# Layer 0's gated product laid out for the out-projection by VectorE blocks and GpSimd copies, and a new order of the last eight granules

## The reference, cut to what matters

```python
def pool_layer(x, norm_g, w_in, w_pool, pool_scale, w_out):      # layer 0
    h = rms_norm(x, norm_g)
    u, z = jnp.split(h @ w_in, 2, axis=-1)                       # 2048 columns each
    y = pool_mixer(u, w_pool, pool_scale) * jax.nn.silu(z)       # windows 2, 4, 8, 16; 4 groups of 512
    return x + y @ w_out

def moba_layer(x, norm_g, w_in, q_norm, k_norm, w_out):          # layer 1
    h = rms_norm(x, norm_g)
    q, k, v, z = jnp.split(h @ w_in, 4, axis=-1)                 # 16 heads of 128 each
    q = rope(rms_norm(heads(q), q_norm))
    k = rope(rms_norm(heads(k), k_norm))
    o = causal_attention(q, k, v)                                # one block of 256 tokens
    return x + (o * jax.nn.silu(z)) @ w_out
```

## Time and profile before

| what | value |
|---|---|
| median of three executions | 426.38 us (426.24 to 426.8) |
| the profiled execution, its own time | 427.27 us |
| its span (first to last instruction) | 425.3 us |
| PE busy | 416.2 us, 98% of the span |
| DVE busy | 292.3 us, 69% |
| ACT busy | 237.0 us, 56% |
| POOL busy | 31.9 us, 8% |
| mean granted clock of TensorE | 0.992 of full |
| moved by DMA | 86.78 MB, mean 204 GB/s |

### The profile page before, as it was taken

One profiled execution on the slowest core, in us unless ns is written; L12 is line 12 of the kernel. 1 busy time (PEld: TensorE's weight loads), 2 busy tenths in 40 slices (PEclk: granted clock), 3 DMA queues, 4 the chain that ended last, 5 costly groups with the idle time before them and its releaser, 6 DMA issues.

```text
span 425.3 us, 5551 instructions
## 1 busy us (share of the span) xinstructions
PE 416.2 (98%) x2126; PEld 356.1 (84%) x2126; DVE 292.3 (69%) x373; ACT 237.0 (56%) x430; POOL 31.9 (8%) x45
## 2 busy tenths in 40 slices
PE   9999999999999999999999999999999999959997
PEld 8989898988888888888888888888888888848885
DVE  3879987779885545358934799358983699833532
ACT  5755453535454443469639785379846797443310
POOL 0175000000000000111001100011001010000000
PEclk9999999999999999999999999999999999988999
DMA  8996868453555747337694567794877927861002
GB/s 269 387 353 213 262 217 322 180 205 114 195 197 168 224 124 222 117 105 241 247 331 119 182 209 236 248 299 147 269 214 215 323 95 272 290 205 50 0 2 99
DMA packets 45945, 86.78 MB, mean 204 GB/s; under 512 B 2528, under 2 KB 8288, under 8 KB 45920
## 3 DMA queue, kind: packets, MB, share of 16 engines
q1 hardware_dynamic: 45200, 85.37, 60.4%
q10 hardware_dynamic: 720, 1.07, 0.8%
HBM read 79.61 MB, written 6.82 MB: 203 GB/s over the span
## 4 chain that ended last, share of the span: by engine, by line
PE 89%; DVE 6%; DMA 3%; SPq 0%; issue 0%; ACT 0%; DVEq 0%
PE acc L633 23%; PE acc L635 23%; PE acc L634 23%; PE acc L656 3%; PE acc L678 3%; PE acc L677 3%; PE acc L675 3%; DMA between<-uT 2%; DVE w_lo L848 2%; PE acc L697 1%; PE aux L688 1%; PE aux L772 1%; PE aux L779 1%; PE aux L771 1%; PE aux L790 1%; PE aux L791 1%
## 5 line engine op out<-in xcount | busy, mean ns | idle before, releaser
L848 DVE TENSOR_TENSOR w_lo<-raw,w_hi 128x2048 fp32r<-128x2048 f32 x65 | 147.9, 2285 | 45.2 <-ACT w_hi L384 45.2
L384 ACT ACTIVATE w_hi<-raw 128x2048 fp32r<-128x2048 f32 x64 | 122.0, 1914 | 43.9 <-PE acc L635 31.0
L633 PE MATMUL acc<-w_hi,hT_hi 128*128 128x512 f32 x320 | 126.9, 397 | 0.0
L635 PE MATMUL acc<-w_hi,hT_lo 128*128 128x512 f32 x320 | 124.8, 390 | 0.0
L634 PE MATMUL acc<-w_lo,hT_hi 128*128 128x512 f32 x320 | 124.6, 389 | 0.0
L635 PEld LDWEIGHTS acc<-w_hi,hT_lo 128*128 128x128 f32 x320 | 60.1, 188 | 12.9
L634 PEld LDWEIGHTS acc<-w_lo,hT_hi 128*128 128x128 f32 x320 | 60.2, 188 | 11.9
L633 PEld LDWEIGHTS acc<-w_hi,hT_hi 128*128 128x128 f32 x320 | 60.1, 188 | 11.7
L633 PE MATMUL acc<-w_hi,aT_hi 128*128 128x512 f32 x160 | 64.7, 404 | 4.9 <-DVE aT_lo L1067 4.9
L634 PE MATMUL acc<-w_lo,aT_hi 128*128 128x512 f32 x160 | 63.2, 395 | 0.0
L635 PE MATMUL acc<-w_hi,aT_lo 128*128 128x512 f32 x160 | 63.1, 395 | 0.0
(11 more groups left out here) (126 smaller groups left out, 452.1 us busy)
## 6 DMA issues: line engine op xcount, KB each, us to landing
raw<-in_w_in_dram SPq DMA_DIRECT2D x46, 1024.0 KB, 6.7
raw<-in_w_out_dram SPq DMA_DIRECT2D x16, 1024.0 KB, 5.3
raw<-in_w_pool_dram SPq DMA_DIRECT2D x4, 1024.0 KB, 5.4
between<-wide SPq DMA_DIRECT2D x8, 512.0 KB, 3.9
raw<-in_w_in_dram SPq DMA_DIRECT2D x8, 256.0 KB, 7.5
wide<-between SPq DMA_DIRECT2D x16, 128.0 KB, 2.8
qkT<-between SPq DMA_DIRECT2D x16, 128.0 KB, 2.9
between<-uT SPq DMA_DIRECT2D x3, 512.0 KB, 10.0
```

The lines of the kernel that those rows point to most:

```text
L384: act.activation(w_hi[:, slot, :], raw[:, slot, :], ACT.Copy).then_inc(hi_made, 1)
L633: pe.matmul(a, shi, whi, start=first and k == 0, stop=False)
L635: ins = pe.matmul(a, slo, whi, start=False, stop=last and k == GK - 1)
L848: dve.tensor_tensor(w_lo[:, slot, :], raw[:, slot, :], w_hi[:, slot, :].bitcast(F32), ALU.subtract).then_inc(w_split, 1)
```

## The change

The transposes of y0 on PE are gone. DVE turns y0 in blocks of 32x32 into `qkT[:, g % 2]`, which holds nothing else at that time, and POOL copies the sixteen 32x256 blocks of a group to their places between the partitions, into the quarter of `wide` that held the group's gate. For that the gate of group g now lies in one contiguous quarter, `quarters[:, g]`. ACT and DVE take the high and the low parts from there, in SBUF, not from PSUM. DVE's list around this is in a new order. In layer 1's out-projection the granule (1, 0) and (1, 1) stand ahead of (0, 2), and the parts of y1 of group 2 are made one round later.

```diff
-OUT1_ORDER = [(0, 0), (0, 1), (0, 2), (1, 0), (1, 1), (1, 2), (0, 3), (1, 3)]
+OUT1_ORDER = [(0, 0), (0, 1), (1, 0), (1, 1), (0, 2), (1, 2), (0, 3), (1, 3)]
...
+        def y0_blocks(g):
+            return qkT[:, g % 2].rearrange("p h s -> p (h s)")
+
+        def y0T(g):
+            return quarters[:, g].rearrange("p t n -> p (t n)").rearrange("p (h s) -> p h s", h=HPG)
...  POOL, behind the rope tables:
+            def place_blocks(dst, blocks, made):
+                for a in range(P // Q):
+                    for b in range(P // Q):
+                        to = dst[b * Q:(b + 1) * Q].rearrange("p h (t a i) -> p a t h i", t=TT, i=Q)[:, a]
+                        at = blocks[a * Q:(a + 1) * Q, b * 2 * P:(b + 1) * 2 * P].rearrange("p (t h i) -> p t h i", t=TT,
+                                                                                            h=HPG)
+                        ins = pool.tensor_scalar(to, at, 1.0, 1.0, ALU.mult, ALU.mult)
+                ins.then_inc(made, 1)
+
+            for g in range(GROUPS):
+                pool.wait_ge(y0_blocked, g + 1)
+                place_blocks(y0T(g), y0_blocks(g), y0T_made)
...  ACT:
             def y0_hi(g):
-                for b in range(2):
-                    turned_hi(aT_hi, HPG * g + 2 * b, 2 * (g % 2) + b, (y_turned, 2 * g + b + 1), y_hi, gain=2 * KD)
-
+                act.wait_ge(y0T_made, g + 1)
+                for h in range(HPG):
+                    f = HPG * g + h
+                    ins = act.activation(aT_hi[:, f, :], y0T(g)[:, h], ACT.Copy,
+                                         scale=gains[:, 2 * KD + f:2 * KD + f + 1])
+                    if h % 2:
+                        ins.then_inc(y_hi, 1)
+
+            static_hi(N_POOL + 4)
             for g in range(GROUPS):
-                if g > 0:
-                    static_hi(N_POOL + 3 + g)
-                    y0_hi(g - 1)
-            static_hi(N_OUT0 + 3)
-            y0_hi(GROUPS - 1)
+                static_hi(N_POOL + 5 + g)
+                y0_hi(g)
...  ACT, last loop:
-                if j == 1:
+                if j == 2:
                     y1_hi(last - 1)
...  PE: turn_y0 and its calls are gone
-                if g > 0:
-                    turn_y0(g - 1)
...
-                    if (half, q) == (0, 0):
-                        turn_y0(GROUPS - 1)
...  DVE:
+            def y0_out(g):
                 for t in range(TT):
                     product_ready(dve, t, 8 + g, N_POOL + g)
                     if g >= 2:
-                        dve.wait_ge(y_turned, 2 * (g - 1))
+                        dve.wait_ge(y0_blocked, g - 1)
                     ins = dve.scalar_tensor_tensor(ysb[:, g % 2, t, :], acc[g % 2][t][:, :], rstd_half[:, t:t + 1],
-                                                   wide[:, t, g * COLS:(g + 1) * COLS], ALU.mult, ALU.mult)
+                                                   quarters[:, g, t, :], ALU.mult, ALU.mult)
                     if t == TT - 1:
                         ins.then_inc(y0_made, 1)
+                dve.wait_ge(y0_made, g + 1)
+                if g >= 2:
+                    dve.wait_ge(y0T_made, g - 1)
+                blocks(y0_blocks(g), ysb[:, g % 2]).then_inc(y0_blocked, 1)
+
+            def y0_lo(g):
+                for h in range(HPG):
+                    f = HPG * g + h
+                    if h % 2 == 0:
+                        dve.wait_ge(y_hi, 2 * g + h // 2 + 1)
+                    ins = dve.scalar_tensor_tensor(aT_lo[:, f, :], y0T(g)[:, h], gains[:, 2 * KD + f:2 * KD + f + 1],
+                                                   aT_hi[:, f, :].bitcast(F32), ALU.mult, ALU.subtract)
+                    if h % 2:
+                        ins.then_inc(y_split, 1)
+
+            dve.wait_ge(gate_made, TT * GROUPS)
+            y0_out(0)
+            weight_lo(N_POOL + 4, (N_POOL + 4) % RING)
+            y0_out(1)
+            weight_lo(N_POOL + 5, (N_POOL + 5) % RING)
+            y0_out(2)
+            y0_lo(0)
+            weight_lo(N_POOL + 6, (N_POOL + 6) % RING)
+            y0_lo(1)
+            y0_out(3)
+            weight_lo(N_POOL + 7, (N_POOL + 7) % RING)
+            y0_lo(2)
+            weight_lo(N_POOL + 8, (N_POOL + 8) % RING)
+            y0_lo(3)
...  DVE, last loop: y1_lo(last - 1) goes from before head_out of j == 1 to behind the weights of j == 2
```

More of the change, by code:

```diff
@@ L192, in bass_hybrid_trunk @@
         tanh_made, gate_made = sem("tanh_made"), sem("gate_made")
-        y0_made = sem("y0_made")
+        y0_made, y0_blocked, y0T_made = sem("y0_made"), sem("y0_blocked"), sem("y0T_made")
         y_turned, y_hi, y_split = sem("y_turned"), sem("y_hi"), sem("y_split")
@@ L444, in layer0 @@
                     product_ready(act, t, 2 * g + 1, 4 * g + 3)
-                    act.activation(wide[:, t, g * COLS:(g + 1) * COLS], acc[1][t][:, :], ACT.Tanh,
+                    act.activation(quarters[:, g, t, :], acc[1][t][:, :], ACT.Tanh,
                                    scale=rstd_half[:, t:t + 1]).then_inc(tanh_made, 1)
@@ L470, in h1_hi @@
                     turned_hi(hT_hi, 4 * half + 2 * b, 2 * half + b, (h_turned, 2 * half + b + 1), h_hi, gain=KD)
-            for n in range(N_OUT0 + 4, N_OUT0 + 8):
+            for n in range(N_OUT0 + 5, N_OUT0 + 8):
                 static_hi(n)
@@ L551, in y1_hi_last @@
                 for b in range(2):
-                    turned_hi(aT_hi, HPG * last + 2 * b, b, (y_turned, 8 + b + 1), y_hi)
+                    turned_hi(aT_hi, HPG * last + 2 * b, b, (y_turned, b + 1), y_hi)
             def layer1(g, attend):
@@ L730, in _ @@
                 layer0(g)
[L733 to L737, removed]
             pe.wait_ge(ident_made, 1)
@@ L943, in layer0 @@
                     dve.wait_ge(tanh_made, TT * g + t + 1)
-                    gate = wide[:, t, g * COLS:(g + 1) * COLS]
+                    gate = quarters[:, g, t, :]
                     ins = dve.scalar_tensor_tensor(gate, gate, 1.0, acc[1][t][:, :], ALU.add, ALU.mult)
@@ L950, in _, with blocks @@
                 layer0(g)
[L952 to L961, removed]
+            def blocks(dst, src):
+                return dve.transpose(dst.rearrange("p (b n i) -> p n b i", b=P // Q, i=Q),
+                                     src.rearrange("p t n -> p (t n)").rearrange("p (n b i) -> p n b i", b=P // Q, i=Q))
+            def y0_out(g):
                 for t in range(TT):
@@ L987, in h1_lo @@
                               gain=KD)
-            for n in range(N_OUT0 + 4, N_OUT0 + 7):
+            for n in range(N_OUT0 + 5, N_OUT0 + 7):
                 weight_lo(n, n % RING)
@@ L1022, in head_out @@
                 ins.then_inc(y1_made, 1)
-            def blocks(dst, src):
-                return dve.transpose(dst.rearrange("p (b n i) -> p n b i", b=P // Q, i=Q),
-                                     src.rearrange("p t n -> p (t n)").rearrange("p (n b i) -> p n b i", b=P // Q, i=Q))
             half = HEAD_DIM // 2
@@ L1114, in _ @@
                     head_max(last, j)
-                if j == 1:
-                    y1_lo(last - 1)
                 if j == 5:
@@ L1123, in _ @@
                     weight_lo(n, n % RING)
+                if j == 2:
+                    y1_lo(last - 1)
             y1_lo_bank(last, 1)
@@ L1127, in _ @@
                     product_ready(dve, t, 30 + half, N_OUT1 + 6 + half)
-                    dve.wait_ge(y_turned, 10)
+                    dve.wait_ge(y_turned, 2)
                     dve.tensor_tensor(ysb[:, half, t, :], acc[half][t][:, :], xs[:, t, half * COLS:(half + 1) * COLS],
```

## The result

The changed kernel takes 431.95 us (median of four, 431.14 to 434.06), the kernel before 426.59 us beside it: ratio 1.0131, 95% interval 1.0088 to 1.0174. It is 5.4 us slower; the prediction had it 0.9 us faster. The time lies in the stated range, on the other side of no change. The profiled execution is the slowest of the four. In this document a median leaves out the executions in a slower state that the chip has (one of four in experiment 2, one of six in the last kernel of experiment 8).

The account below looks back on a forecast made before the run. PE's list plus its waits was taken to bound the kernel; -7.3 us from the order and +6.4 us in y0's stage (holding the -3.5 of PE's turns) gave -0.9 us: 425.5 us, range 415.6 to 434 us.

Parts of the forecast that it names:

- the first case: Granules 20 to 23: POOL at its rows' copy price, held by DVE, is the bound; 425.5 us, chance 0.44.
- The third case: POOL's y0 copies take clearly more than their rows say: +4.2 us at 0.45 us a copy, +10.6 at 0.55; chance 0.26.
- the pattern and the move: POOL's copies: three-dimensional pattern and change of partitions, in no row, might raise the price to 0.55 us.
- PE's turns: Four y0 turns of eight transposes, 0.87 us each, leave PE's list: 3.5 us shorter.
- the second case: POOL's y0 copies are hidden, wholly or nearly, and PE has no wait: 415.6 us, or some 420; chance 0.26.
- The order: Layer 1's out-projection: the new order removes a 4.9 us wait and 2.4 us of slow clock, 7.3 us.
- The price of a copy: A 32x256 POOL copy takes 0.37 us from start to start, 23.7 us in all.
- The holds: DVE operations with two SBUF inputs hold POOL: four w_lo at 2.05 us, twelve low parts at 0.2 us.
- The clock behind the last wait: After PE's last y0 wait, ahead of granule 23: zero cost for a lowered clock, up to 2.4 us in the range.
- PE's waits: PE waits 10.3 us for y0, in four pieces of 1 to 4 us ahead of granules 20 to 23.
- The sum: POOL done at 143.8 us, granule 23 ending at 151.8, stage 6.4 us longer; with -7.3 us, -0.9 us in all.
- The rule weighed: POOL's cores each go on once their share is done, so four copies of different quadrants could run at once.

Follow-up runs that it names:

- experiment 2: Changed kernel with the out-projection's old order and the old places of y1's parts, so only y0's new way: 438.87 us, ratio 1.025 to the kernel before.
- experiment 8: Changed kernel, fewer y0 groups by GpSimd: mixed (1 and 3 by PE) 417.98, again 418.23 us; last kernel (GpSimd and ScalarE, only 3 by PE) 417.61 us.
- experiment 6: Changed kernel with four contiguous 128x256 GpSimd copies a group instead of sixteen 32x256, no move between partitions, y0 laid out wrongly: 416.35 us.
- experiment 1: Kernel before with only the new order of layer 1's out-projection and later parts of y1's group 2, y0 as before: 420.04 us, ratio 0.9835.
- experiments 4 and 5: Changed kernel with copies kept in their partitions (427.28 us) or contiguous (434.16 us), both with y0 wrong; then with the two copy loops exchanged (432.97 us).
- experiment 3: Changed kernel with VectorE's five w_lo of the stage reading their second input from PSUM instead of SBUF, low parts wrong: 421.1 us.
- experiment 7: Changed kernel with six of each group's sixteen copies on ScalarE and group 3's y0 earlier: 420.25 us; the same with loops exchanged: 420.2 us.

## Why the prediction was wrong, point by point

The mechanism of the first case is what happened; two terms of its sum were too small. The first of them alone turns the sign: GpSimd was done 4.4 us later than the sum had it, and -0.9 + 4.4 = +3.5 us. The third case, a copy of 0.45 us or more, is the one that came true: it had 0.26, and +4.2 us for 0.45 us. Its two reasons, the pattern and the move, are not what made the copies dear.

- **PE's turns, -3.5 us: right.** With GpSimd in time (experiment 6) the kernel is at 416.35 us, near the second case's 415.6.
- **The order, -7.2 to -7.3 us: right**, alone (experiment 1) and beside the other part (experiment 2). All of it is the wait and the slow clock behind it.
- **The price of a copy, 0.37 us: wrong, the first failed term.** It is 0.46 us. The tensor_scalar rows gave the 0.40 us of busy time well; the step from one to the next was taken from operations on the same 128 partitions, which start 0.04 us before the last one ends. Where the partitions change, they start 0.06 us after it (experiments 4 and 5). 64 x 0.09 = 5.8 us. I had put the price's risk in the pattern and in the move. The pattern costs nothing, and the move adds nothing to the change (0.46 us with and without it); a move without a change was not run.
- **The holds: right.** Five of 2.02 us (experiment 3) where the sum had four of 2.05 and a start 2 us later. The low parts were set too dear, at 0.2 us each; they cost about 0.07 (0.47 us beside them, 0.40 without), 1.4 us less in all. GpSimd's last copy was done at 148.2 us where the sum had 143.8: 5.8 - 1.4 = 4.4.
- **High and low parts of group 3: right**, 2.7 us for 2.6.
- **The clock behind the last wait, 0 with 2.4 us in the range: wrong, the second failed term.** Granule 23 took 8.5 us until it was done instead of 5.44: 3.1 us, above the 2.4 of the range too. I had set zero since the waits would mostly be shorter than the 2.9 us of idle time ahead of the only fall in the trace of before. But the last wait, the one that counts, was 3.47 us, and the clock fell after those of 2.19 and 2.41 us as well. Of the four executions two took 431.1 us; that these were spared the last fall fits their spans, 3 us shorter, at a mean clock of 0.988, but no row here shows it.
- **PE's waits, 10.3 us forecast and 10.4 measured: luck.** The forecast had no slow stretch between the waits. Granules 20 and 21, which ran in part at the lower clock, took 7.4 us each up to the next wait, granule 22 took 5.7; what they took longer came off the waits behind them.
- **The sum.** 4.4 + 0.1 + 3.1 = 7.6 us: from the predicted 151.8 to the 159.4 us at which granule 23 was done.
- **The lists of ACT, DVE and SP: right.** PE has no wait for weights in granules 24 to 27.
- **The rule weighed.** The Trainium skill, GPSIMD Engine Reference, section 2.1, says that each core goes on with the next instruction once its share of the one before is done. From it I took that copies on different partitions could run at once. The rows don't bear that out: with the partitions changing at each copy the step is the longest of all, with 0.06 us between two copies. They show whole instructions and no single core, so what the rule says of the cores stays open.
- **The range.** Its upper end is not a copy of 0.49 us: -0.9 + 64 x 0.12 = +6.8 is 433.2 us, and 434 belongs to 0.50.

The wrong choice was one of weight. A stage that by its own sum makes PE wait for 10 us has no slack, so an error in the price counts 64 times: from 0.37 us to the upper figure of 0.55 us it is 11.5 us, against a forecast gain of 0.9.

## What to carry to other kernels

Before work goes from the bottleneck to an idle engine, count that engine's instructions against the deadline of each consumer, not against its idle share: POOL was 8% busy before the change, and PE still waited 10 us for it, since sixteen short instructions and a hold took 9 to 10 us where PE makes a granule in 5.44. If the engine can't keep the pace, give it every second piece: with half of the turns left to PE the kernel takes 14 us less than with all of them moved, though only 2 us less than with none moved (experiments 8 and 1). And two parts that hide each other's result should be timed alone: here one changed the time by -7 us and the other by +12.

## What the runs showed of the hardware that was not expected

- A GpSimd tensor_scalar of 32x256 float32 is busy for 0.40 us. The next starts 0.37 us after it if it reads and writes the same partitions, and 0.46 us after it if either changes (experiments 4 and 5).
- One of 128x256 has the same shortest duration, 0.40 us (experiment 6).
- The granted clock fell to its lower level after waits of PE of 2.19 and 2.41 us and not after another of 2.34 us, all three in the profiled execution of the changed kernel.
- A VectorE operation of 2.25 us with both inputs in SBUF holds a GpSimd copy for 2.02 us; with one of them in PSUM it takes as long and holds none (experiment 3). A block turn of 1.25 us, with its one input in SBUF, holds none either: beside the one at 111.03 us in the changed kernel the copy at 111.38 us took 0.39 us.
- ScalarE can make the same copy between partitions: six in 2.55 us in the kernel of experiment 7.
